# RG-LRU gates: both gates of a channel block in one 64x128 stationary, pairs of matmuls on the two row halves; turn of the normed rows behind the query projection

## The reference, cut to what matters

```python
xc, conv_new = _causal_conv(xa, conv0, conv_w, conv_b)
xb = x.reshape(B, L, N_BLK_A, BLK_A)          # 8 blocks of 64 channels
r = sigmoid(einsum('blnc,ncd->blnd', xb, wa).reshape(B, L, D_A) + ba)
i = sigmoid(einsum('blnc,ncd->blnd', xb, wx).reshape(B, L, D_A) + bx)
log_a = -8 * softplus(-lam) * r
a = exp(log_a)
u = sqrt(maximum(-expm1(2 * log_a), 0)) * (i * x)
h = associative_scan((a, u))                  # h_t = a_t h_{t-1} + u_t
ya = h * silu(ga)
...
yb = rmsnorm(ob, onorm_w) * silu(gb)
m = concatenate([ya, yb]) @ w_out
x = x + gate * rmsnorm(m, post_w)
```

## Time and profile before

| | us |
|---|---|
| three timed runs | 954.93, 958.16, 958.32 (median 958.16) |
| profiled execution, its own time | 956.15 |
| span of that execution in the profile | 954.3 |
| one inner body (n = 1 to 6), start to start | 103.30 |

### The profile page before, as it was taken

The page is one execution under the profiler, slowest core; times in us unless marked ns, Lnnn a source line. Parts: engine busy times, 40 slices in busy tenths (PEclk is TensorE's granted clock), DMA queues, the critical chain, the costliest instruction groups (busy, mean ns, idle before and its releaser), DMA issues.

```text
span 954.3 us, 20981 instructions
## 1 busy us (share of the span) xinstructions
PE 886.7 (93%) x8178; PEld 651.7 (68%) x8235; DVE 680.3 (71%) x1791; ACT 511.2 (54%) x1057; POOL 259.3 (27%) x348
## 2 busy tenths in 40 slices
PE   4789967899999999999999999999999999999884
PEld 4647856459775887579665977588757966597742
DVE  2576795758777786867686877778686768677766
ACT  2555559534764358535753476435853575336631
POOL 6032254702232121412140223212141214022300
PEclk9999987999999999999999999999999999999998
DMA  9996111100110000100110011000010101010134
GB/s 313 324 346 223 45 34 56 67 1 23 46 67 2 23 24 23 67 2 24 45 67 2 24 45 68 1 23 28 19 67 1 46 1 53 2 46 1 59 118 139
DMA packets 46910, 61.19 MB, mean 64 GB/s; under 512 B 2845, under 2 KB 40561, under 8 KB 46813
## 3 DMA queue, kind: packets, MB, share of 16 engines
q1 hardware_dynamic: 46812, 59.86, 18.9%
HBM read 48.90 MB, written 10.95 MB: 63 GB/s over the span
## 4 chain that ended last, share of the span: by engine, by line
PE 54%; DVE 19%; ACT 12%; issue 7%; DMA 2%; POOL 2%; SPq 2%; DVEq 0%; ACTq 0%; POOLq 0%
PE ring L431 44%; DVE xc L1349 5%; DVE qlo L1252 2%; DVE kk L1270 2%; ACT hnh L1002 2%; PE okv L520 2%; PE okv L522 1%; PE okv L521 1%; DVE qq L1268 1%; ACT aux L999 1%; ACT okv L999 1%; DMA wol<-in_ada_w_dram 1%; SPq L356 1%; DVE xc L1347 1%; POOL wol L1761 1%
## 5 line engine op out<-in xcount | busy, mean ns | idle before, releaser
L431 PE MATMUL ring<-hnh,wih 128*128 128x256 bf16 (+1 forms) x1152 | 289.6, 263 | 2.4 <-DVE hnl L1391 2.2
L431 PE MATMUL ring<-hnl,wih 128*128 128x256 f16 (+1 forms) x1152 | 289.5, 262 | 0.0
L431 PE MATMUL ring<-hnh,wil 128*128 128x256 bf16 (+1 forms) x1152 | 289.4, 262 | 0.0
L431 PE MATMUL ring<-woh,work 128*128 128x512 f16 x512 | 162.4, 379 | 1.3
L1774 POOL TENSOR_TENSOR klo<-kk,khi 128x256 bf16<-128x256 f32 x96 | 75.2, 784 | 227.7 <-ACT khi L914 227.2
L431 PEld LDWEIGHTS ring<-hnh,wih 128*128 128x128 f16 x1152 | 110.1, 98 | 15.5 <-DVE hnl L1391 2.8
L431 PEld LDWEIGHTS ring<-hnl,wih 128*128 128x128 f16 x1152 | 110.1, 98 | 12.1
L431 PEld LDWEIGHTS ring<-hnh,wil 128*128 128x128 bf16 x1152 | 110.1, 98 | 11.8
L1252 DVE TENSOR_TENSOR qlo<-qq,qhi 128x256 f16<-128x256 f32 x112 | 66.3, 592 | 67.4 <-ACT qhi L918 58.0
L914 ACT ACTIVATE khi<-kk 128x256 f16<-128x256 f32 x96 | 40.3, 420 | 113.9 <-DVE kk L1270 87.3
L431 PE MATMUL ring<-wih,hnh 128*128 128x512 f16 x256 | 97.7, 382 | 2.4 <-ACT kk L897 1.3
(11 more groups left out here) (356 smaller groups left out, 1904.8 us busy)
## 6 DMA issues: line engine op xcount, KB each, us to landing
xin<-in_x_prompt_dram SPq DMA_DIRECT2D x16, 512.0 KB, 3.6
work<-in_x_prompt_dram SPq DMA_DIRECT2D x16, 512.0 KB, 4.3
out_dram<-work SPq DMA_DIRECT2D x16, 512.0 KB, 2.6
work<-in_ada_w_dram SPq DMA_DIRECT2D x4, 1024.0 KB, 8.2
woh<-in_ada_w_dram SPq DMA_DIRECT2D x4, 1024.0 KB, 12.9
wol<-in_w_in_dram SPq DMA_DIRECT2D x4, 1024.0 KB, 12.1
work<-in_w_in_dram SPq DMA_DIRECT2D x4, 1024.0 KB, 10.5
woh<-in_w_in_dram SPq DMA_DIRECT2D x4, 1024.0 KB, 9.8
```

The lines of the kernel that those rows point to most:

```text
L431: last = mm(out, a(k), b(k), start=start and k == ks[0] and j == 0, stop=stop and k == ks[-1] and j == 2)
```

## The change

`wg` has half its size. For each channel group c, the partitions 0 to 63 hold the two gate blocks of the even block side by side (r, then i), and partitions 64 to 127 those of the odd block (i, then r), so that no part of it is zero; the clearing by GpSimd and SP's wait for it are gone. `gates` makes for each c two matmuls of 64 rows x 128 columns by 256, one on each half of the array's rows, into the two aux banks. Each bank now holds 64 partitions of r and 64 of i. All four are released to ACT together (`g_ps`), and all wait for `kt_sb` first. `gates_out` takes each 64-partition piece out on its own: four Sigmoids for r and four for i, where there were two and two. The i pieces are written to other partitions than they are read from. In the decode part the same is done with 32 columns: 8 ACT instructions become 16.

In `body`, PE's wait for `i_sig` of the previous body ahead of FR becomes one for the squares of older output rows (`esq`), and `turn_y` moves behind the Q projection and waits for `i_sig` there. `turn_x(n + 1, 0)` waits for `i_sig` instead of `r_sig`.

```diff
-        wg = sb("wg", [P, 2, CT, P])
+        wg = sb("wg", [P, CT, P])
...
             def gates(n, p):
                 pe.wait_ge(cvc.sem, cvc.at(n, 8 * p + 8))
-                for w, s in ((0, gr_ps), (1, gi_ps)):
-                    if p == 0 and w == 0:
...
-                    elif w == 1:
-                        if n == 0 and p == 0:
-                            pe.wait_ge(gate_ok, 1)
-                        pe.wait_ge(kt_sb.sem, kt_sb.at(n, p + 1))
-                    elif n < BODIES - 1:
-                        pe.wait_ge(hn_lo.sem, hn_lo.at(n + 1, 2))
-                    for c in range(2):
-                        last = mm(aux[(1 + w + p) % 2][:, T * c:T * c + T], wg[:, w, 2 * p + c, :], xc[:, p, c, :],
-                                  start=True, stop=True)
-                    last.then_inc(s.sem, 1)
+                if p == 0:
...
+                elif n < BODIES - 1:
+                    pe.wait_ge(hn_lo.sem, hn_lo.at(n + 1, 2))
+                pe.wait_ge(kt_sb.sem, kt_sb.at(n, p + 1))
+                for c in range(2):
+                    for odd in range(2):
+                        k = slice(HALF * odd, HALF * odd + HALF)
+                        last = mm(aux[odd][:, T * c:T * c + T], wg[k, 2 * p + c, :], xc[k, p, c, :], start=True, stop=True)
+                last.then_inc(g_ps.sem, 1)
...
                 weights(1)
-                if not first:
-                    pe.wait_ge(i_sig.sem, i_sig.at(n - 1, 4))
+                if n == 1:
+                    pe.wait_ge(gp_sb, 2)
+                elif n > 1:
+                    pe.wait_ge(esq[0].sem, esq[0].at(n - 2, 2))
                 project(ring[0], FR, 0, n)
                 project(ring[0], FR, 1).then_inc(fr_ps.sem, 1)
+                weights(2)
+                if n > 1:
+                    pe.wait_ge(esq[1].sem, esq[1].at(n - 2, 2))
+                project(ring[1], Q_, 0)
+                project(ring[1], Q_, 1).then_inc(q_ps.sem, 1)
                 if not first:
                     turn_y(n - 1, 0)
                     turn_y(n - 1, 1)
-                weights(2)
-                project(ring[1], Q_, 0)
-                project(ring[1], Q_, 1).then_inc(q_ps.sem, 1)
...
             def gates_out(n, p):
-                act.wait_ge(gr_ps.sem, gr_ps.at(n, p + 1))
+                act.wait_ge(g_ps.sem, g_ps.at(n, p + 1))
                 act.wait_ge(iu.sem, iu.at(n, p))
                 for c in range(2):
-                    A(rr[:, c, :], aux[(1 + p) % 2][:, T * c:T * c + T], ACT.Sigmoid,
-                      bias=pcol("ba", 2 * p + c)).then_inc(r_sig.sem, 1)
-                act.wait_ge(gi_ps.sem, gi_ps.at(n, p + 1))
+                    for odd in range(2):
+                        k, src = slice(HALF * odd, HALF * odd + HALF), aux[odd][:, T * c:T * c + T]
+                        ins = A(rr[k, c, :], src[k, :], ACT.Sigmoid, bias=pcol("ba", 2 * p + c)[k, :])
+                    ins.then_inc(r_sig.sem, 1)
                 act.wait_ge(scan.sem, scan.at(n, 2 * p))
                 for c in range(2):
-                    A(ii[:, c, :], aux[p][:, T * c:T * c + T], ACT.Sigmoid, bias=pcol("bx", 2 * p + c)).then_inc(i_sig.sem, 1)
+                    for odd in range(2):
+                        k, o = slice(HALF * odd, HALF * odd + HALF), slice(HALF * (1 - odd), HALF * (1 - odd) + HALF)
+                        ins = A(ii[k, c, :], aux[odd][o, T * c:T * c + T], ACT.Sigmoid, bias=pcol("bx", 2 * p + c)[k, :])
+                    ins.then_inc(i_sig.sem, 1)
```

More of the change, by code:

```diff
@@ L41 @@
 P = 128
+HALF = P // 2
 D = 1024
@@ L182, in build @@
         u_ps = Signal("u_ps", 4)
-        gr_ps, gi_ps = Signal("gr_ps", 2), Signal("gi_ps", 2)
+        g_ps = Signal("g_ps", 2)
         f_sig, k_sig, q_sb = Signal("f_sig", 2), Signal("k_sig", 2), Signal("q_sb", 2)
@@ L357, in _ @@
                 if (kind, c) == ("ada", 7):
-                    sp.wait_ge(zeroed, 1)
                     for w, src in ((0, rg_wa), (1, rg_wx)):
@@ L361, in _ @@
                             v = src[0].rearrange("(t two) c d -> two c t d", two=2)[odd]
-                            sp.dma_start(wg[64 * odd:64 * odd + 64, w, :, 64 * odd:64 * odd + 64], v).then_inc(wg_ld, 16)
+                            col = HALF * (w ^ odd)
+                            sp.dma_start(wg[HALF * odd:HALF * odd + HALF, :, col:col + HALF], v).then_inc(wg_ld, 16)
             def residual(n, t):
@@ L476, in turn_y @@
                     pe.wait_ge(yb_ok.sem, yb_ok.at(n, 8))
-                    pe.wait_ge(r_sig.sem, r_sig.at(n, 4))
-                else:
                     pe.wait_ge(i_sig.sem, i_sig.at(n, 4))
@@ L526, in gates @@
                 pe.wait_ge(cvc.sem, cvc.at(n, 8 * p + 8))
[L527 to L542 removed]
+                if p == 0:
+                    if n == 0:
+                        pe.wait_ge(wg_ld, 64)
+                        pe.wait_ge(gate_ok, 1)
+                    else:
+                        pe.wait_ge(ytl.sem, ytl.at(n - 1, 4))
+                elif n < BODIES - 1:
[6 more added lines that the diff above has]
+                last.then_inc(g_ps.sem, 1)
             def ada(i, bank):
@@ L694, in body @@
                 level(n, 1, 6)
-                pe.wait_ge(r_sig.sem, r_sig.at(n, 2))
+                pe.wait_ge(i_sig.sem, i_sig.at(n, 2))
                 if not last_body:
                     turn_x(n + 1, 0)
-                    pe.wait_ge(i_sig.sem, i_sig.at(n, 2))
                     turn_x(n + 1, 1)
@@ L755, in _ @@
             turn_mod(3, ring[1], 0)
-            pe.wait_ge(zeroed, 3)
+            pe.wait_ge(zeroed, 2)
             pe.wait_ge(carry_zero, 2)
@@ L833, in _ @@
             pe.wait_ge(dv("conv_d"), 16)
-            for w in range(2):
-                for c in range(CT):
-                    o = TD * CT * w + TD * c
-                    last = mm(lev[1][:, o:o + TD], wg[:, w, c, :], xcd[:, TD * c:TD * c + TD], start=True, stop=True)
+            for c in range(CT):
+                for hf in range(2):
+                    k = slice(HALF * hf, HALF * hf + HALF)
+                    last = mm((lev[1], aux[0])[hf][:, TD * c:TD * c + TD], wg[k, c, :], xcd[k, TD * c:TD * c + TD],
+                              start=True, stop=True)
             last.then_inc(dv("gates_ps"), 1)
@@ L1173, in _ @@
                 for c in range(CT):
-                    o = W4 * w + TD * c
-                    A(dst[:, TD * c:TD * c + TD], lev[1][:, o:o + TD], ACT.Sigmoid, bias=pcol(bias, c)).then_inc(dv("ri_d"), 1)
+                    cols = slice(TD * c, TD * c + TD)
+                    for hf in range(2):
+                        k, o = slice(HALF * hf, HALF * hf + HALF), HALF * (hf ^ w)
+                        ins = A(dst[k, cols], (lev[1], aux[0])[hf][o:o + HALF, cols], ACT.Sigmoid, bias=pcol(bias, c)[k, :])
+                    ins.then_inc(dv("ri_d"), 1)
             act.wait_ge(dv("ri_d"), 2 * CT)
@@ L1575, in _ @@
             rest(2)
-            dve.wait_ge(zeroed, 3)
+            dve.wait_ge(zeroed, 2)
             body(0, True, False)
@@ L1821, in _ @@
                             base=0, channel_multiplier=1).then_inc(ident_ok, 1)
-            G.memset(wg[:, :, :, :], 0.0).then_inc(zeroed, 1)
             G.memset(khi[1][:, :], 0.0).then_inc(sets_zero, 1)
```

## The result

| | before | changed |
|---|---|---|
| median of the runs, us | 958.24 (954.93 to 960.07) | 991.23 (990.81 to 991.9) |
| ratio | | 1.036, 95% interval 1.0342 to 1.0377 |
| span of the profiled execution, us | 954.3 | 989.7 |
| one inner body, us | 103.30 | 107.90 |

The changed kernel is 3.6% slower. The sign and the place were as predicted, the size was not: 35.4 us of span are added where the sum said 16.6, and 991 lies outside the range of 963 to 982.

A forecast was written before the change was run, and what follows sets the result against it. A DVE and ACT chain was taken to bound each body from 437 to 470.6 us, PE after that. 1.87 + 6 x (1.45 + 0.74) + 0.78 + 0.8 = 16.6 us on 956.15 gave 972.7, said as 973, range 963 to 982.

The forecast's parts named there:

- The sign: Whole kernel: the change was said to make it slower, 973 us against 956.15 in the profiled execution.
- the place: ACT's Sigmoids in gates_out: first call +1.45 us a body ahead of PE's unit, second +0.74 at next body's level 0.
- the sum: All terms over body 0, six inner bodies, body 7 and decode: 16.6 us added; chance 0.53.
- a bound on a cost: Gate Sigmoids in gates_out: at most 2.5 us added a call instead of 1.45; the range counted 1.05 more on seven bodies.

The follow-up runs named there:

- x1: The kernel before with each Sigmoid of the gates cut at partition 64, halves alternating low, high, low, high; ratio 1.0416.
- x2: The kernel before with each Sigmoid of the gates cut at partition 64, halves paired low, low, high, high; ratio 1.0306.
- x3: The kernel before with each Sigmoid of the gates cut by columns into two of 128 partitions x 128 elements; 964.51 us, ratio 1.0083.
- x7: The kernel before with the first gates_out call moved behind xa_out and the heads of level 6, exponentials behind level 7's heads, POOL's order following; 959.59 us, ratio 1.003.
- x11: The kernel before with only the moved turn_y and the waits for esq in place of i_sig; 954.86 us against 957.41, ratio 0.9968.
- x9: The changed kernel with only the first gates_out call of a body cut into halves, the second taking whole banks; 979.14 us, ratio 1.0222.
- x4: The changed kernel with the body's Sigmoids taking whole banks, r and i mixed, decode's 16 still cut; 957.99 us, ratio 1.0021.

## What to carry over

Before an instruction is cut by partitions, look for the distance of starts and not only for the duration, and look for it where neighbours work on different partitions: these neighbours were cheap only because they overlapped. A packing that saves PE 0.87 us where it waits anyway, and makes ACT, which is on the chain, take the results out in pieces, is paid on ACT, twice a body. When a bound on a cost goes into a range, count it as often as the cost stands in the sum. And when a bundle of edits loses, its parts are worth running alone: here moving one group of transposes past a projection and dropping a wait that was not needed there gave 0.3% by themselves.

## What the runs showed of the hardware

- **ACT's overlap depends on the partitions of its neighbour.** PSUM to SBUF Sigmoids of 256 elements start 0.36 us apart on 128 partitions and 0.37 on one 64-partition half. They start 0.47 to 0.49 us apart where the half that is read or the half that is written changes. With 32 columns it is 0.18 on 128 partitions and 0.30 with halves in turn. The loss is 0.10 to 0.13 us for each change.
- **It need not be the half.** The copies of L1193 do not overlap even from partition 0 to partition 32, both in the low half, though an instruction on 128 partitions and the copy on 8 behind it do (935.89 and 935.98). All these rows would fit a loss wherever the first partition changes. No run was made to test that.
- **Two 64-row float32 matmuls on the two row halves overlap in full:** two begin nearly together every 0.22 us, 128 recorded instructions in 19.1 us against 33.1 with 128 rows, same columns.
- **PE's clock fell in single bodies, behind the unit.** Between 200 and 895 us it fell in one to three bodies of x1 and of each kernel with packed gates, and in none of before, x2, x3, x7 and x11. In body 5 of the changed kernel PE was idle for 3.88 us in four pieces in the 13 us before, as in its other bodies, where the clock stayed up. The stretch (length, busy times, clock 0.67) mixes the levels of 2.4 GHz (1.00) and 1.2 GHz:

```profile
700.00:705.00 5.00, 5.00 (x27) 3.78 (x26) 1.30 (x3) 4.82 (x10) 0.00 (x0) 0.67 0.00 0
```

  That body has 107.90 us like all others: the waits for k_sig and level 0 behind it, 0.81 + 1.18 us in the others, are 0.50 us here and swallow the loss. In x9, where these waits are missing, the body with the fall has 107.23 us and the others 105.59:

```profile
531.95:639.18 107.23, 103.22 (x866) 74.22 (x865) 76.67 (x202) 59.93 (x129) 26.70 (x33) 0.98 0.09 31
639.18:744.77 105.59, 101.58 (x867) 73.03 (x865) 76.67 (x202) 59.74 (x129) 26.68 (x33) 1.00 0.09 31
```

  In x4 it is 104.52 against 102.85. So one fall costs about 1.65 us where nothing hides it; in x1, whose PE waits for `i_sig` behind it, it is 109.78 against 108.63. Which body it hits, and why kernels with much the same idle time are spared, stays open.
